# Stick-breaking z: gated inside its head and stored gated, with one product and one subtraction per tile left for the gate phase

## The reference

```python
proj = einsum('bsd,de->bse', rmsnorm(x, norm_g), w_in)     # 9 groups of columns, the last 2048 wide
sb_q, sb_k, sb_v, sb_z, hg_q, hg_f, hg_i, hg_z, gate_logits = split(proj)
sb_o = sb_attention(sb_q, sb_k, sb_v)                      # 8 heads of 128
u_sb = einsum('bse,ed->bsd', sb_o * silu(sb_z), w_sb_proj)
hg_o = rmsnorm(hgrn2(silu(hg_q), 1 - f, log f, hg_i), hg_norm_g)
u_hg = einsum('bse,ed->bsd', hg_o * silu(hg_z), w_hg_proj)
gates = sigmoid(gate_logits + b_gate)
y = gates[:, :1024] * u_sb + gates[:, 1024:] * u_hg
out = rmsnorm(x + y @ w_out, final_norm_g)
```

## Time and profile before

| | |
|---|---|
| median of 3 runs | 1443.66 us (1442.77 to 1444.6) |
| the profiled execution's own time | 1442.67 us |
| its span, first to last instruction | 1440.6 us |
| mean granted TensorE clock | 0.979 |
| TensorE busy | 1355.1 us, 94% |
| VectorE busy | 959.2 us, 67% |
| ScalarE busy | 577.1 us, 40% |
| GpSimd busy | 709.6 us, 49% |

### The profile page before, as it was taken

The page is one execution under the profiler, slowest core; times in us unless marked ns, Lnnn a source line. Parts: engine busy times, 40 slices in busy tenths (PEclk is TensorE's granted clock), DMA queues, the critical chain, the costliest instruction groups (busy, mean ns, idle before and its releaser), DMA issues.

```text
span 1440.6 us, 23216 instructions
## 1 busy us (share of the span) xinstructions
PE 1355.1 (94%) x8408; PEld 1122.2 (78%) x8408; DVE 959.2 (67%) x1074; ACT 577.1 (40%) x958; POOL 709.6 (49%) x488
## 2 busy tenths in 40 slices
PE   5689999999999999999999999999898979999998
PEld 4568778778878878878878887887776768888886
DVE  4827976976977886896797697687533275545323
ACT  8336255346335535634634634543423321111131
POOL 6655744654565554564574465555556522223210
PEclk8799999999999999999999999999989989999999
DMA  5121121112111121121112111122343475433512
GB/s 147 29 74 30 60 86 32 61 45 71 62 30 59 46 74 59 30 89 59 30 61 73 45 61 45 58 74 89 103 158 105 151 241 177 154 95 116 192 44 102
DMA packets 134348, 119.41 MB, mean 83 GB/s; under 512 B 10096, under 2 KB 116592, under 8 KB 134256
## 3 DMA queue, kind: packets, MB, share of 16 engines
q1 hardware_dynamic: 125040, 92.84, 20.5%
q10 hardware_dynamic: 9216, 25.17, 5.1%
HBM read 88.63 MB, written 29.36 MB: 82 GB/s over the span
## 4 chain that ended last, share of the span: by engine, by line
PE 66%; DVE 12%; issue 9%; ACT 4%; POOL 4%; DMA 4%; SPq 0%; DVEq 0%; POOLq 0%; ACTq 0%
PE banks L1506 32%; PE banks L1756 12%; PE banks L1778 6%; PE banks L1584 4%; PE banks L1563 3%; DMA w_raw<-in_w_in 3%; DVE hk L1040 3%; PE banks L1574 2%; POOL b_lo L568 2%; POOL b_sum L568 2%; DVE forget L1040 1%; DVE hq L1040 1%; DVE scT L1272 1%; PE banks L1643 1%; DVE scT L1244 1%
## 5 line engine op out<-in xcount | busy, mean ns | idle before, releaser
L1506 PE MATMUL banks<-a_hi,b_hi 128*128 128x512 f32 x1120 | 468.4, 418 | 37.7 <-POOL b_lo L568 17.4
L1506 PE MATMUL banks<-a_hi,b_lo 128*128 128x512 f32 x1120 | 445.5, 398 | 0.0
L1506 PE MATMUL banks<-a_lo,b_hi 128*128 128x512 f32 x1120 | 444.5, 397 | 0.0
L568 POOL TENSOR_TENSOR b_lo<-w_raw,b_hi 128x512 fp32r<-128x512 f32 x120 | 183.0, 1533 | 300.8 <-ACT b_hi L656 291.7
L1506 PEld LDWEIGHTS banks<-a_hi,b_hi 128*128 128x128 f32 x1120 | 215.3, 192 | 86.2 <-POOL b_lo L568 19.9
L1506 PEld LDWEIGHTS banks<-a_hi,b_lo 128*128 128x128 f32 x1120 | 214.3, 191 | 48.1
L1506 PEld LDWEIGHTS banks<-a_lo,b_hi 128*128 128x128 f32 x1120 | 215.7, 193 | 37.5
L568 POOL TENSOR_TENSOR b_lo<-b_sum,b_hi 128x512 fp32r<-128x512 f32 x120 | 176.8, 1474 | 129.1 <-ACT b_hi L656 129.1
L1142 DVE TENSOR_TENSOR_SCAN kappa<-kappa 128x128 f32<-128x128 f32 (+3 forms) x64 | 97.0, 1516 | 100.8 <-ACT kappa L773 100.8
L656 ACT ACTIVATE b_hi<-b_sum 128x512 fp32r<-128x512 f32 x120 | 75.5, 631 | 136.9 <-POOL b_sum L568 136.9
L640 POOL TENSOR_TENSOR w_lo<-w_raw,w_hi 128x1024 fp32r<-128x1024 f32 x20 | 48.1, 2409 | 153.7 <-ACT w_hi L656 153.7
(11 more groups left out here) (194 smaller groups left out, 2467.7 us busy)
## 6 DMA issues: line engine op xcount, KB each, us to landing
w_raw<-in_w_in SPq DMA_DIRECT2D x80, 512.0 KB, 5.0
gate_d<-gate_out SPq DMA_DIRECT2D x16, 512.0 KB, 3.6
gate_in<-gate_d ACTq DMA_DIRECT2D x32, 256.0 KB, 2.9
x_tok<-in_x SPq DMA_DIRECT2D x8, 512.0 KB, 6.1
z_d<-z_out SPq DMA_DIRECT2D x8, 512.0 KB, 2.7
hz_d<-z_out SPq DMA_DIRECT2D x8, 512.0 KB, 2.7
osb_d<-o_sb SPq DMA_DIRECT2D x8, 512.0 KB, 5.7
ohg_d<-hq SPq DMA_DIRECT2D x8, 512.0 KB, 2.7
```

The source lines that it names most:

```text
L568: return nc.gpsimd.tensor_tensor(dst, a, b, op)
L1506: last = mm(bank, w[:, s, k, :], t[s][:, k, :], start=opens and k == 0 and z == 0, stop=k == QUAD - 1 and z == 2, skip_group_check=not opens)
```

## The change

z is gated in its own head. At the last point of `first_half` ScalarE makes z_sig, the sigmoid of z_out. VectorE multiplies z_out by it at the start of `second_half`, between `normalize` and the first `weigh`. SP stores the product: `store_z` waits for it (z_silu), and so does ScalarE before the scores of tile 1, since beta1 lies where z_sig lies. In the gate phase a tile takes one product on VectorE (`gate_osb`, now VectorE's), a copy on ScalarE for the high part (`osb_high`, point 9 of pair g = e + 2) and one subtraction on VectorE (`osb_low`). Tiles 6 and 7 are done inside the last pair. ScalarE's fetch of the first HGRN tile no longer waits for VectorE's steps.

```diff
@@ -160,6 +160,8 @@
         u2 = place("u2", block_at(0), [HALF])
         u3 = place("u3", block_at(0) + 2 * KB, [HALF])
         z_out = place("z_out", block_at(1), [S])
+
+        z_sig = place("z_sig", block_at(13), [S])
         v_tok = place("v_tok", block_at(2), [NT, P])
         k_hi = place("k_hi", block_at(3), [S], F32R)
         k_lo = place("k_lo", block_at(4), [S], F32R)
...
@@ -437,16 +442,21 @@
                 sp.wait_ge(hg_norm, h + 1)
                 sp.dma_start(ohg_d[h], hq[:, :]).then_inc(hg_stored, 16)
 
-            def store_z(h, pair, dst):
-                sp.wait_ge(block_taken, 5 * (4 * h + pair) + 4)
-                sp.dma_start(dst[h], z_out[:, :]).then_inc(z_stored, 16)
+            def store_z(h):
+
+                sp.wait_ge(z_silu, h + 1)
+                sp.dma_start(z_d[h], z_out[:, :]).then_inc(z_stored, 16)
+
+            def store_hz(h):
+                sp.wait_ge(block_taken, 5 * (4 * h + 3) + 4)
+                sp.dma_start(hz_d[h], z_out[:, :]).then_inc(z_stored, 16)
 
             def step(h, after):
                 load_head_pair(h, 1)
                 if after:
                     store_sb(h - 1)
                 load_head_pair(h, 2)
-                store_z(h, 1, z_d)
+                store_z(h)
                 load_head_pair(h, 3)
                 if after:
                     store_hg(h - 1)
...
@@ -762,6 +772,9 @@
 
             def sigmoids(h, j):
                 n = (j + 1) * P
+                if j == 1:
+
+                    act.wait_ge(z_silu, h + 1)
                 act.wait_ge(qk_done, 8 * h + j + 1)
                 n_banks, m = score_banks(j)
                 score = banks[:, 4:4 + n_banks, 0:m]
...
@@ -831,6 +844,9 @@
                         k_split(h)
                     if u == 14:
                         q_split(h)
+                    if u == POINTS - 1:
+                        act.wait_ge(block_taken, 5 * n + 4)
+                        nc.scalar.activation(z_sig[:, :], z_out[:, :], ACT.Sigmoid).then_inc(z_sig_done, 1)
                     if attend:
                         if u in I_AT:
                             g = I_AT[u]
...
@@ -897,18 +913,14 @@
                 act.wait_ge(block_taken, 5 * (N_HEAD_PAIRS + g) + 5)
                 make_gate(g, 0, slice(HALF, S), gate_out[0][:, HALF:S]).then_inc(gate_made[0], 1)
 
-            def fetch_osb(e, dst_z):
+            def fetch_osb(e):
                 act.dma_start(osb_raw[e][:, :], osb_d[e]).then_inc(osb_loads(e)[0], 16)
-                act.dma_start(dst_z[:, :], z_d[e]).then_inc(osb_loads(e)[0], 16)
-
-            def z_of_osb(e):
-                return z_last if e == KT - 1 else (z_in[0], gate_flat)[e % 2]
-
-            gate_flat = gate_in[:, :, :].rearrange("p a n -> p (a n)")
-
-            def gate_osb(e):
-                act.wait_ge(*osb_loads(e))
-                nc.scalar.activation(osb_sig[e][:, :], z_of_osb(e)[:, :], ACT.Sigmoid).then_inc(oz_sig, 1)
+                act.dma_start(osb_gate[e][:, :], z_d[e]).then_inc(osb_loads(e)[0], 16)
+
+            def osb_high(e):
+
+                act.wait_ge(osb_gated, e + 1)
+                copy(osb_hi[e][:, :], osb_raw[e][:, :]).then_inc(osb_hi_ready, 1)
 
             def fetch_ohg(e):
                 act.dma_start(ohg_raw[e][:, :], ohg_d[e]).then_inc(ohg_loads(e)[0], 16)
...
@@ -947,32 +959,26 @@
                     if p == 12:
                         act.wait_ge(block_taken, 5 * n + 4)
                         make_gate(g, 1, slice(0, S), gate_out[1][:, :]).then_inc(gate_made[1], 1)
-                    if 1 <= g <= KT - 2:
-                        e = g - 1
-                        if p == 3:
-                            if e == 0:
-                                act.wait_ge(sb_stored, 16 * HEADS)
-                                act.wait_ge(z_stored, 16 * 2 * HEADS)
-                            if e == 1:
-                                act.wait_ge(hg_stored, 16 * HEADS)
-                            need(act, oz_step, 2 * e - 3)
-                            fetch_osb(e, z_of_osb(e))
-                        if p == 10:
-                            gate_osb(e)
+                    if 1 <= g <= KT - 2 and p == 3:
+                        if g == 1:
+                            act.wait_ge(sb_stored, 16 * HEADS)
+                            act.wait_ge(z_stored, 16 * 2 * HEADS)
+                        if g == 2:
+                            act.wait_ge(hg_stored, 16 * HEADS)
+                        fetch_osb(g - 1)
+                    if g >= 2 and p == 9:
+                        osb_high(g - 2)
                     if final:
                         if p == 3:
 
                             act.wait_ge(product_done, done + P1 + 1)
-                            act.wait_ge(oz_step, 2 * (KT - 4) + 1)
-                            fetch_osb(KT - 2, z_of_osb(KT - 2))
-                        if p == 6:
-                            act.wait_ge(product_done, done + P7 + 1)
-                            fetch_osb(KT - 1, z_of_osb(KT - 1))
-                        if p == 10:
-                            gate_osb(KT - 2)
+                            fetch_osb(KT - 2)
+                            fetch_osb(KT - 1)
                         if p == 11:
-                            gate_osb(KT - 1)
+                            osb_high(KT - 2)
                             split_panel(0, w_hi[:, 0, :, :])
+                        if p == 12:
+                            osb_high(KT - 1)
             finish_gate(N_GATE_PAIRS - 1)
 
             for i in range(2):
...
@@ -982,13 +988,9 @@
                 for b in range(2):
                     if t > 0:
                         act.wait_ge(gated, 2 * (t - 1) + b + 1)
-                    else:
-
-                        act.wait_ge(oz_step, 2 * (KT - 3) + 1)
                     act.dma_start(gate_in[:, b, :], halfs(gate_d[t], b)).then_inc(gate_loaded[b], 16)
 
             act.wait_ge(product_done, PRODUCTS * N_PAIRS)
-            act.wait_ge(oz_step, 2 * KT)
             fetch_ohg(0)
             fetch_gate(0)
             fetch_ohg(1)
...
@@ -1321,6 +1323,8 @@
                 n = 4 * h + 2
                 if attended_before:
                     normalize(h - 1)
+                dve.wait_ge(z_sig_done, h + 1)
+                tt(z_out[:, :], z_out[:, :], z_sig[:, :], ALU.mult).then_inc(z_silu, 1)
                 weigh(h, 0)
                 weigh(h, 1)
                 take_u2(QF_PAIR, n)
...
@@ -1381,24 +1385,26 @@
             dve.wait_ge(pv_done, 8 * HEADS)
             dve.wait_ge(z_stored, 32 * HEADS)
 
-            def silu_split(e, loads, raw, z, sig, hi, lo, split_done, done_before):
-
-                dve.wait_ge(*loads(e))
-                first = 2 * (done_before + e)
-                tt(raw[e][:, :], raw[e][:, :], z, ALU.mult).then_inc(oz_step, 1)
-                dve.wait_ge(oz_step, first + 1)
-                dve.wait_ge(oz_sig, done_before + e + 1)
-                tt(raw[e][:, :], raw[e][:, :], sig[e][:, :], ALU.mult).then_inc(oz_step, 1)
-                dve.wait_ge(oz_step, first + 2)
-                v.tensor_copy(hi[e][:, :], raw[e][:, :]).then_inc(o_hi_ready, 1)
-                dve.wait_ge(o_hi_ready, done_before + e + 1)
-                tt(lo[e][:, :], raw[e][:, :], hi[e][:, :].bitcast(F32), ALU.subtract).then_inc(split_done, 1)
-
-            gate_flat = gate_in[:, :, :].rearrange("p a n -> p (a n)")
-
-            def split_osb(e):
-                z = z_last if e == KT - 1 else (z_in[0], gate_flat)[e % 2]
-                silu_split(e, osb_loads, osb_raw, z[:, :], osb_sig, osb_hi, osb_lo, osb_split, 0)
+            def gate_osb(e):
+                dve.wait_ge(*osb_loads(e))
+                tt(osb_raw[e][:, :], osb_raw[e][:, :], osb_gate[e][:, :], ALU.mult).then_inc(osb_gated, 1)
+
+            def osb_low(e):
+                dve.wait_ge(osb_hi_ready, e + 1)
+                tt(osb_lo[e][:, :], osb_raw[e][:, :], osb_hi[e][:, :].bitcast(F32), ALU.subtract).then_inc(osb_split, 1)
+
+            def split_ohg(e):
+
+                raw, z = ohg_raw[e][:, :], z_in[e % 2][:, :]
+                dve.wait_ge(*ohg_loads(e))
+                tt(raw, raw, z, ALU.mult).then_inc(ohg_step, 1)
+                dve.wait_ge(ohg_step, 2 * e + 1)
+                dve.wait_ge(ohg_sig_done, e + 1)
+                tt(raw, raw, ohg_sig[e][:, :], ALU.mult).then_inc(ohg_step, 1)
+                dve.wait_ge(ohg_step, 2 * e + 2)
+                v.tensor_copy(ohg_hi[e][:, :], raw).then_inc(ohg_hi_ready, 1)
+                dve.wait_ge(ohg_hi_ready, e + 1)
+                tt(ohg_lo[e][:, :], raw, ohg_hi[e][:, :].bitcast(F32), ALU.subtract).then_inc(ohg_split, 1)
 
             a = HEADS - 1
             n = N_HEAD_PAIRS
...
@@ -1432,14 +1438,20 @@
                 n += 1
                 take_u2(n, n)
                 take_u3(n, n)
+                gate_osb(g - 2)
                 dve.wait_ge(gate_stored[1], 16 * g)
                 take_c22(GATE_PAIR, n)
```

(26 more changed lines are left out.)

10 lines of the change are left out of this document (5 added, 5 removed).

## The result

The changed kernel takes 1461.99 us by the median of 4 runs (1460.94 to 1463.4), the kernel before 1443.8 us (4 runs). The ratio is 1.013, with a 95% interval of 1.0118 to 1.0142: 18.2 us slower. The forecast was 1453.8 us in a range of 1447 to 1460, so the sign was right and the time lies above the range, at what the first rival gave (1461 to 1464).

A forecast was written before the change was run, and what follows sets the result against it. TensorE was taken as the bound nearly everywhere, except a gate-phase ring without it. Heads 3.9, head 0 1.1, ring 2.8 and hand-over 2.3 sum to +10.1 us on 1442.67; with 1.0 for the median, 1453.8, range 1447 to 1460.

The forecast's parts named there:

- the first rival: Heads: late loads push ScalarE and with it score tiles 3 to 5; 7 to 10 us more, 1461 to 1464, chance 0.12.
- The late loads: Heads: loads behind the z store leave later, ScalarE slips 1 to 2 us, cost to TensorE taken as 0.
- the sign that would show the forecast wrong: A gate pair at 24.3 us or less, no new wait at the turn, or TensorE waits at turns 3 to 5.
- The product before the first turn: Heads 1 to 7: VectorE's z product delays the first weights, TensorE waits; 0.55 us a head, +3.9 us.
- Head 0: Head 0: the z product meets GpSimd's last low parts, on which TensorE's wait hangs; +1.1 us (0 to 1.3).
- The ring: Gate phase, load to sums to next load without TensorE: slip less two gains, +2.8 us (+0.1 to +3.3).
- 6.5 of slip: Gate pairs g = 2 to 6: P5's low part on GpSimd meets osb_low, next load 1.3 us later, five times.
- The meetings gone: Gate phase: the old osb_lo no longer meets GpSimd right after each load; -2.75 us.
- The sigmoid gone from g = 1: Gate pair g = 1: no sigmoid ahead of the square root on which normalization, store and load hang; -0.95 us.
- The hand-over: Into the HGRN branch: a wait for the late gate store replaces that for VectorE's passes; +2.3 us (1.0 to 3.5).
- The other advice that was weighed: Gate phase: move work to ScalarE only when VectorE is saturated; with the copy on VectorE no ring slip, sum +3.6 us.

The follow-up runs named there:

- the fourth experiment: The changed kernel, with VectorE taking c12 and c21 ahead of gated blocks 6 and 7 and their low parts in the last gate pair: 1458.65 us.
- the first experiment: The changed kernel, with SP issuing the loads of the head's last projection pair ahead of the store of z: 1456.61 us.

## Why the prediction missed

- **The late loads: the failed step.** The prediction said that ScalarE slips 1 to 2 us at w_raw, that the next weights TensorE needs from this are some 15 us away, "and I take 0". The idle time at w_raw was 2.80 us in head 6. The weights were indeed not late; what was late was wT, which stands in ScalarE's in-order queue behind the high part of t, and t is late by w_raw and by three GpSimd sums that are now the ones to wait for VectorE (2.19 + 2.46 + 1.76 for 3 x 1.28, 2.6 us more). Measured 8.4 us over the heads, shown by the loads moved back, and nearly all of it in heads 2 to 6. This was rival 1, with the right size (7 to 10 us) and a chance of 0.12, and the sign that would show the forecast wrong came: TensorE waits at turn 4. Only the way to TensorE was another, the copy wT and not a score tile. The rival was denied with 2 to 3 us between a score tile and its user; the margin that counted, between the copy wT and the end of the turn of tile 4, was 1.0 us in the kernel before, and no row of the prediction has it.
- **The product before the first turn.** 0.55 a head, +3.9; measured 4.6 to 5.0 by two experiments, 0.66 to 0.71 a head, at the forecast place and by the forecast mechanism: TensorE waits 0.4 to 0.5 us at the turn seven times. What was too small is the refill, 0.25 us a head in place of 0.05.
- **Head 0.** +1.1; the wait for v_tok grew by 0.9, as GpSimd's two low parts took 3.49 us for 2.61. By the z store it is 1.9 in all. The rest goes with a lower clock: between 79 and 105 us the granted clock was 0.87 in all eight profiles with the change or a part of it, and 0.93 in both without. In stretches of 2 us it is 0.50 (1.2 of 2.4 GHz) from 97 to 99 and then 0.87 before, and 0.50 from 97 to 101 and then 0.66 after, both times just behind TensorE's wait for v_tok. No term of the sum stood for it. The product does not explain it, since it was 0.87 with the product left out too, where the wait for v_tok was 5.0. Why the clock is lower there stays open.
- **The ring.** 6.5 of slip; 124.03 less the 117.4 of the two kernels without it are 6.6. The meetings gone, -2.75: 117.4 against 119.55 are -2.2. The sigmoid gone from g = 1, -0.95: -0.94. In sum 3.5 for 2.8. A pair was foretold near 25; four take 25.0 to 25.2 and the first 23.5. P5's low part was foretold near 1.9, it is 1.81; TensorE's wait at over 4, it is 4.3. The Trainium skill, page "SBUF — State Buffer", section "Who interferes with whom", had let VectorE's two-input instruction and GpSimd shut each other out; the slip that this gave (1.3 us) and not the one without it (0.75 in the text, 0.8 by its own two times) is what the trace shows.
- **The hand-over.** +2.3; measured 2.0, and the wait for y_sum is 4.1 (foretold near 5). VectorE took the last block at 1183.59; in the fourth experiment TensorE released it 13.22 us after the last ring load, which would be 1176.89 here, so it lay there for 6.7 us (foretold some 7). The prediction then had the rest run as before; it took 0.7 us more, with the granted clock at 0.80 for 0.88.
- The other advice that was weighed, to leave the cast on VectorE (the Trainium skill, "Perfetto Trace Analysis", "Optimizing Scalar/DVE Operations"), got its number: with the cast on VectorE the ring is 6.75 us shorter, with ScalarE at an earlier point 6.5. The cast took 0.68 us on VectorE and the copy 1.05 on ScalarE, as the page has it, but that difference is not what the ring felt: the advice gave the right sign for the place chosen, and another place on ScalarE did as well.

With the late loads at their measured 8.4 the same sum would have given 1462.2. That it comes so near the 1461.99 is in part luck: the other terms measured 12.4 us in the profile (5.0 + 1.9 + 3.5 + 2.0) and not 10.1, and the two profiled executions lie 20.15 us apart where the medians lie 18.2.

## What to carry to other kernels

When a step in an in-order queue is given a new wait, follow every instruction behind it to the engine that consumes it, and then that engine's queue as well: what became late here was not what the load feeds, but an attention copy that happened to stand behind it. A cover of a few microseconds that hangs on an engine whose instructions stretch beside another engine's (1.28 to 2.46 us here) must be counted with the stretched durations; a small shift in time can change which of the two has to wait. A pass given to a less busy engine belongs where its data is ready and that engine would wait for a load; the same operation cost 6.5 us in five pairs at one point, against four points earlier, where it did as well as on the other engine.

## What was not expected of the hardware

- GpSimd's sum of 128x512 took 2.46 us, near twice its 1.28, beside VectorE's scan of 128x640, which had started 0.10 us earlier and took 1.49. In the kernel before and in the first experiment GpSimd's t started 0.01 and 0.03 us ahead of the same scan: then t took 1.28 us and the scan 2.61 and 2.60. Whichever started first ran at its own time, and the other took over a microsecond more.
- Of two weight loads of 512 KB issued right behind a store of 512 KB, the later took 6.9 to 7.0 us to land in heads 2 to 6, where the median of these loads is 5.1 us. Another store (of the HGRN output) was issued right behind them; no run tells the two stores' parts apart.
- The granted clock after the hand-over was 0.76 to 0.88 over 14 us in seven of the ten profiles and 1.00 in three, and the stretch behind y_sum was 1.5 to 2.9 us shorter in those three.
